# Two score tiles instead of one in every chunk of the gate building, each row whole behind four quads

## The chip, the cores and the metric

The program runs on one core of a Trainium2 chip. The metric is the device time of one execution in microseconds (us), lower is better. The engines are TensorE (PE), VectorE (DVE), ScalarE (ACT), GpSimd (POOL) and SyncE (SP, which here only issues weight loads).

## The reference

Two blocks over 512 tokens of width 1024 in float32. The first block has two layers (feed-forward, mixer, feed-forward), the second one a mixer and then a layer of 16384 experts. Only this last layer, `_peer`, is touched:

```python
qry = (t @ w_q).reshape(n_tok, 8, 2, 128)
scores = einsum("thpd,hpkd->thpk", qry, sub_keys)
s_top, i_top = top_k(scores, 16)              # per half key
cand = s_top[..0..] + s_top[..1..]; best, pos = top_k(cand, 16)
gate = softmax(best)                          # 8 heads x 16 experts a token
act = gelu(tb . u_tab[idx]); out = sum((gate * act) * v_tab[idx])
```

The kernel does not gather experts. It computes the score of all 16384 experts for all tokens as a dense product with u_tab, applies gelu, multiplies by a dense gate matrix that is zero where an expert was not chosen, and takes the dense product with v_tab.

## The kernel before

**Weights.** All weights come as tiles of 128 x 2048 floats (1 MB). SP loads a tile into `raw`, two slots in turn, as soon as the slot's low part has been taken. ACT copies it into `w_hi` in a reduced format (`split_hi`, L427), POOL computes the rest `w_lo = raw - w_hi` in four pieces (L390), and PE forms every product three times: high by high, high by low, low by high (`product`, L925 to L927). A tile of u_tab holds two score rows of 128 experts each; a row is 8 blocks times 3 matmuls, 24 matmuls of 128 x 512, and so a tile is 48. The queue of ACT is in order: `split_hi` of tile n + 2 stands right behind the issue of the store of tile n.

**Groups.** The 128 score rows are 32 groups (`GROUPS`) of four rows, two u tiles and two v tiles each. The scores of the first `AHEAD` = 18 groups, 36 tiles, are computed ahead, before the gates are there: PE fills bank e (0 or 1) with a row (`ahead_row`), ACT applies gelu into `stage` (`stage_row`, L740), and stores the tile of two rows to DRAM (`store_tile`, `s_store`, L745). They are read back per group into `s_in` (L809). The places of the 36 tiles are: 24 between the top-k steps (6 behind each of four key score blocks, `CHOICE_TILES`), 8 in the gate building, one for every chunk, and 4 behind it (`last` to `last + 3`). While those 4 run, the first groups of gates are loaded.

**Gate building.** A quad is four tokens. DVE writes the one-hot operands of a quad (`hots`: four tensor_scalar, L2410, and one tensor_tensor, L2413) into one of four buffers of `hot`, PE makes its gates in one of four banks (`quad`, L1631; the profile shows 8 matmul records for a quad), ACT copies the bank to `g_buf` (L785). DVE waits for quad q - 4 before it overwrites a buffer, PE waits for the copy of quad q - 4 before it overwrites a bank. A chunk is 16 quads (64 tokens); there are 8. PE runs four quads, then half a row (12 matmuls), four times for a chunk. At the end of a chunk ACT issues the store of 4 MB of gates (`g_store`, L791), and right behind it the store of the score tile and `split_hi`:

```python
                        stage_row(CHOICE_TILES * TT + c, half)
                    c_ev.held()
                    act.dma_start(g_store[:, c] ..., g_buf[:, c % 2] ...)
                    store_tile(CHOICE_TILES * TT + c)
```

**Groups of the experts.** An early group (g below `AHEAD`) costs PE two v tiles only (`v_products`), and loads 1 MB of gates, 1 MB of scores and 2 MB of weights. A late group costs PE two u tiles (`s_products`) and two v tiles. DVE multiplies scores by gates (`weigh`, L2441), ACT and DVE split the product (L825, L2448), DVE adds the result to `x` (L2460).

Of the kernel before, what the change touches and what calls it, by code (L numbers as in the profile page):

```python
# [29 lines left out]
TT = TOKENS // P  # L30
# [30 lines left out]
GROUPS = NKEYS // EG  # L61
CHUNK = 64
CHUNKS = TOKENS // CHUNK
AHEAD = 18
AHEAD_TILES = 2 * AHEAD
CHOICE_TILES = 6
QUAD_BUFS = 4
# [48 lines left out]
def build(nc, x_in, weights, gains, small, pool_w, consts, rope, second, level_masks,  # L116
# [3 lines left out]
    with stack:  # L120
# [15 lines left out]
        def sem(name):  # L136
            if name not in sems:
                sems[name] = stack.enter_context(nc.semaphore(name))
            return sems[name]
# [193 lines left out]
        def u_tile(g):  # L333

            return TABLE_AT + (2 * g if g < AHEAD else 4 * g - 2)

        def v_tile(g):

            if g < AHEAD - 1:
                return TABLE_AT + AHEAD_TILES + 2 * g  # L340
# [62 lines left out]
        def _(act):  # L403
# [15 lines left out]
            def split_hi(tile, i=None, per=2):  # L419

                if i is None and tile >= TILES:
                    return
                slot, half = tile % 2, tile // 2
                act.wait_ge(tile_landed[slot], 16 * (half + 1) if i is None else i * (8 * per) + 16 * (half + 1))
                if tile >= 2:
                    act.wait_ge(tile_used, tile - 1 if i is None else i * per + (tile - 1))
                act.activation(w_hi[:, slot, :], raw[:, slot, :], ACT.Copy).then_inc(hi_written, 1)  # L427
# [257 lines left out]
            def experts():  # L685
# [44 lines left out]
                def stage_row(n, e, i=None):  # L730

                    if e == 0:
                        act.wait_ge(sem("s_ahead_done"), n + 1 if i is None else i * 2 + (n + 1))
                        if n >= 2:

                            there = 16 * (n // 2)
                            act.wait_ge(s_stored[n % 2], there if i is None else i * 16 + there)
                    else:
                        act.wait_ge(tile_used, TABLE_AT + n + 1 if i is None else i * 2 + (TABLE_AT + n + 1))
                    c_st.up(act.activation(stage[:, n % 2, e, :], banks[e][:, :], ACT.Gelu))  # L740

                def store_tile(n, i=None):
                    target = n if i is None else act.snap(i * 2 + n)
                    c_st.held()
                    act.dma_start(s_store[target], stage[:, n % 2]).then_inc(s_stored[n % 2], 16)  # L745
                    split_hi(TABLE_AT + n + 2, i)
# [7 lines left out]
                for t in range(TT):  # L754
                    n = CHOICE_TILES * t
# [16 lines left out]
                for c in range(CHUNKS):  # L772
                    for half in range(2):
                        with act.Fori(0, CHUNK // 32) as i:
                            c_ev.loop(i, 4)
                            for b in range(4):
                                q = CHUNK // 4 * c + CHUNK // 8 * half + b
                                at = act.snap(i * 16 + (CHUNK // 2 * half + 4 * b))
                                act.wait_ge(sem("quad_done"), i * 4 + (q + 1))

                                if c >= 2:
                                    act.wait_ge(stored[c % 2], 16 * (c // 2))
                                else:
                                    act.wait_ge(sem("keys_landed"), 32)
                                c_ev.up(act.activation(  # L785
                                    g_buf[:, c % 2, :, bass.ds(at, 4)],
                                    banks[quad_banks[b]][:, :].rearrange("p (t i) -> p i t", t=4), ACT.Copy))
                        c_ev.end(CHUNK // 32)
                        stage_row(CHOICE_TILES * TT + c, half)
                    c_ev.held()  # L790
                    act.dma_start(g_store[:, c].rearrange("g j n -> j g n"),  # L791
                                  g_buf[:, c % 2].rearrange("p (g e) t -> p g (e t)", g=GROUPS)).then_inc(stored[c % 2], 16)
                    store_tile(CHOICE_TILES * TT + c)


                landed = [sem("gates_landed0"), sem("gates_landed1")]
# [2 lines left out]
                def load_group(g, i=None):  # L799
# [3 lines left out]
                    if g >= 2 or i is not None:  # L803
# [3 lines left out]
                                  g_store[source].rearrange("c j n -> j c n")).then_inc(landed[g % 2], 16)  # L807
                    if g < AHEAD:
                        act.dma_start(s_in[:, g % 2].rearrange("p (a e) t -> p a (e t)", a=2),  # L809
# [3 lines left out]
                def chain(g, e, i=None):  # L813
                    at = EG * g + e + 1 if i is None else i * (2 * EG) + (EG * g + e + 1)
                    if g >= AHEAD:

# [3 lines left out]
                        else:  # L820
                            done = 2 * (g - AHEAD) + e // 2 + 1
                            act.wait_ge(sem("s_done"), done if i is None else i * 4 + done)
# [35 lines left out]
                        c.end(trips)  # L858


                last = CHOICE_TILES * TT + CHUNKS
                assert AHEAD_TILES == last + 4
                ahead(last)
                ahead(last + 1)
# [32 lines left out]
            for layer in range(LAYERS):  # L897
                ffn(2 * layer)
                mix(layer)
                ffn(2 * layer + 1)  # L900
            second_mixer()
            experts()

        @block.tensor
        def _(pe):
# [16 lines left out]
            def product(out_ap, slot, blk, m_hi, m_lo, start, stop):  # L922

                cols = slice(blk * P, blk * P + P)
                pe.matmul(out_ap, w_hi[:, slot, cols], m_hi, start=start, stop=False)  # L925
                pe.matmul(out_ap, w_hi[:, slot, cols], m_lo, start=False, stop=False)  # L926
                return pe.matmul(out_ap, w_lo[:, slot, cols], m_hi, start=False, stop=stop)  # L927
# [8 lines left out]
            def wait_tile(tile, i=None, per=2):  # L936
                pe.wait_ge(lo_written, tile + 1 if i is None else i * per + (tile + 1))
# [602 lines left out]
            def experts():  # L1540
# [38 lines left out]
                def ahead_row(n, e, part, i=None):  # L1579

                    tile = TABLE_AT + n
                    if part == 0:
                        if e == 0:
                            wait_tile(tile, i)
                        if n > 0:

                            at = 2 * (n - 1) + e + 1
                            pe.wait_ge(sem("s_staged"), at if i is None else i * 4 + at)
                    for r in range(KB // 2 * part, KB // 2 * (part + 1)):
                        if n == 0 and e == 0 and i is None:  # L1590
                            pe.wait_ge(sem("h_lo_written"), KB * (k + 1) + r + 1)
                        last = product(banks[e][:, :], tile % 2, KB * e + r, h_hi[:, r, :], h_lo[:, r, :],
                                       r == 0, r == KB - 1)
                    if part == 1:
                        (used if e else c_sa).up(last)

                def ahead(n, i=None):
                    for e in range(2):
                        for part in range(2):
                            ahead_row(n, e, part, i)  # L1600

                key_scores(0)
                for t in range(TT):
                    n = CHOICE_TILES * t
# [19 lines left out]
                def quad(q, i=None):  # L1624
                    pe.wait_ge(sem("hot_written"), q + 1 if i is None else i * PER_TRIP + (q + 1))
                    if q >= QUAD_BUFS:

                        at = q - QUAD_BUFS + 1
                        pe.wait_ge(sem("quad_stored"), at if i is None else i * PER_TRIP + at)
                    for n in range(4):  # L1630
                        ins = pe.matmul(banks[quad_banks[q % 4]][:, n * P:n * P + P], hot[:, q % 4, n, 1, :],  # L1631
                                        hot[:, q % 4, n, 0, :], start=True, stop=True)
                    c_quad.up(ins)

                PER_TRIP = 2 * CHUNK // 4

                def two_chunks(c, i=None):

                    for m in range(2):
                        for part in range(4):  # L1640
                            for n in range(4):
                                quad(CHUNK // 4 * (c + m) + 4 * part + n, i)
                            ahead_row(CHOICE_TILES * TT + c + m, part // 2, part % 2, i)

                two_chunks(0)
                with pe.Fori(0, (CHUNKS - 2) // 2) as i:
                    c_quad.loop(i, PER_TRIP)
                    used.loop(i, 2)
                    c_sa.loop(i, 2)
                    two_chunks(2, i)  # L1650
                for c in (c_quad, used, c_sa):
                    c.end((CHUNKS - 2) // 2)


                def s_products(g, i=None):
# [26 lines left out]
                                           w_mix_lo[:, g % 2, e, :], e == 0, e == EG - 1)  # L1682
                        (used if d % 4 == 3 else c_v).up(last)

                for n in range(CHOICE_TILES * TT + CHUNKS, AHEAD_TILES):
                    ahead(n)


# [956 lines left out]
```

## Time and profile before

| | us |
|---|---|
| median of 3 runs | 4459.71 (4449.06 to 4461.06) |
| the profiled execution's own time | 4452.29 |
| its span in the profile | 4450.5 |
| PE busy | 4218.7 (95%) |
| DVE busy | 1950.5 (44%) |
| POOL busy | 1795.3 (40%) |
| ACT busy | 1313.2 (30%) |
| mean granted TensorE clock | 0.974 of full speed |

The span is the time between the first and the last recorded event; the execution's own time has 1.8 us around it. PE's busy time counts a matmul from its start to its modelled end, and neighbours overlap, so the spacing of starts tells the cost of one, not the mean duration.

### The profile page before, as it was taken

The numbers are of one execution on the slowest core, as the hardware profiler recorded it, in microseconds if no ns is written. First come the engines' busy times: TensorE is split into PE (matmuls) and PEld (weight loads), VectorE is DVE, ScalarE is ACT, GpSimd is POOL, SyncE is SP. The second block draws the span as 40 slices with busy tenths as digits, with TensorE's granted clock in tenths as the row PEclk, the third lists the DMA queues.
The fourth block names the chain that finished last, engine by engine and source line by source line (L and its number), as shares of the span: only waits on it lengthen the run. The fifth ranks groups of instructions, "written<-read, shape, count | busy, mean of one in ns | idle before, by whom it ended". The sixth has DMA issues, their size and how long they took to land.

```text
span 4450.5 us, 54686 instructions
## 1 busy us (share of the span) xinstructions
PE 4218.7 (95%) x20004; PEld 3501.2 (79%) x20004; DVE 1950.5 (44%) x3700; ACT 1313.2 (30%) x1599; POOL 1795.3 (40%) x1328
## 2 busy tenths in 40 slices
PE   8999899999999999999987889999888999999998
PEld 6888668888888777887866878787787888888887
DVE  2213443212212443211387763695884666333333
ACT  3222243223222143222231123333333222222322
POOL 4444234444444334444320014445113555554553
PEclk9999999999999999999998999999999999999999
DMA  3222112222222112223110002333456555333332
GB/s 123 95 104 88 64 69 95 94 96 93 95 103 97 67 67 85 94 96 108 57 48 1 1 20 105 109 128 133 154 177 217 193 194 195 126 113 132 113 123 76
DMA packets 127504, 461.30 MB, mean 104 GB/s; under 512 B 8080, under 2 KB 73872, under 8 KB 84752
## 3 DMA queue, kind: packets, MB, share of 16 engines
q1 hardware_dynamic: 48960, 351.29, 22.1%
q10 hardware_dynamic: 78416, 108.22, 7.0%
q8 instruction: 90, 1.47, 0.1%
q14 instruction: 38, 0.31, 0.0%
HBM read 404.96 MB, written 54.53 MB: 103 GB/s over the span
## 4 chain that ended last, share of the span: by engine, by line
issue 51%; POOL 25%; PE 23%; DVE 0%; POOLq 0%; ACT 0%; ACTq 0%; DVEq 0%
POOL w_lo L390 25%; PE bank L925 8%; PE bank L926 8%; PE bank L927 8%; POOLq L394 0%; DVE x L2511 0%; POOLq L397 0%; DVE weighed L2441 0%; DVE w_mix_lo L2448 0%; DVE sq_last L1759 0%; PE bank L967 0%; PE bank L960 0%; ACT stage L740 0%; POOLq L390 0%; DVE sq_last L1760 0%
## 5 line engine op out<-in xcount | busy, mean ns | idle before, releaser
L390 POOL TENSOR_TENSOR w_lo<-raw,w_hi 128x512 fp32r<-128x512 f32 x1324 | 1795.1, 1387 | 2621.7 <-ACT w_hi L427 2621.6
L925 PE MATMUL bank<-h_hi,w_hi 128*128 128x512 f32 x3232 | 1283.6, 397 | 53.6 <-POOL w_lo L390 26.9
L926 PE MATMUL bank<-h_lo,w_hi 128*128 128x512 f32 x3232 | 1267.6, 392 | 0.0
L927 PE MATMUL bank<-h_hi,w_lo 128*128 128x512 f32 x3232 | 1267.5, 392 | 0.0
L427 ACT ACTIVATE w_hi<-raw 128x2048 fp32r<-128x2048 f32 x331 | 632.4, 1911 | 1207.9 <-PE bank L927 1129.8
L925 PEld LDWEIGHTS bank<-h_hi,w_hi 128*128 128x128 f32 x3232 | 613.7, 190 | 189.2 <-issue 50.1
L927 PEld LDWEIGHTS bank<-h_hi,w_lo 128*128 128x128 f32 x3232 | 612.4, 189 | 130.6
L926 PEld LDWEIGHTS bank<-h_lo,w_hi 128*128 128x128 f32 x3232 | 614.0, 190 | 127.4 <-issue 1.8
L925 PE MATMUL bank<-w_mix_hi,w_hi 128*128 128x512 f32 x1024 | 398.4, 389 | 0.9 <-ACT stage L740 0.9
L927 PE MATMUL bank<-w_mix_hi,w_lo 128*128 128x512 f32 x1024 | 398.3, 389 | 0.0
L926 PE MATMUL bank<-w_mix_lo,w_hi 128*128 128x512 f32 x1024 | 398.3, 389 | 0.0
L2460 DVE TENSOR_TENSOR x<-x,bank 128x512 f32<-128x512 f32 x256 | 172.6, 684 | 299.8 <-PE bank L927 298.2
L925 PE MATMUL bank<-act_hi,w_hi 128*128 (+1 forms) x704 | 273.9, 389 | 0.0
L926 PE MATMUL bank<-act_lo,w_hi 128*128 (+1 forms) x704 | 273.9, 389 | 0.0
L927 PE MATMUL bank<-act_hi,w_lo 128*128 (+1 forms) x704 | 273.9, 389 | 0.0
L1774 DVE SCALAR_TENSOR_TENSOR x<-bank,x 128x512 f32<-128x512 f32 x56 | 38.1, 681 | 453.5 <-PE bank L927 453.5
L1802 DVE TENSOR_TENSOR up_s<-bank,rstd 128x512 f32<-128x512 f32 x88 | 60.9, 692 | 383.1 <-PE bank L927 382.9
L925 PEld LDWEIGHTS bank<-w_mix_hi,w_hi 128*128 128x128 f32 x1024 | 192.2, 188 | 41.4 <-issue 1.3
L927 PEld LDWEIGHTS bank<-w_mix_hi,w_lo 128*128 128x128 f32 x1024 | 192.2, 188 | 39.8
L926 PEld LDWEIGHTS bank<-w_mix_lo,w_hi 128*128 128x128 f32 x1024 | 192.2, 188 | 39.8
L456 ACT ACTIVATE act_hi<-up_s 128x512 f32 (+1 forms) x88 | 55.6, 631 | 461.2 <-DVE up_s L1804 461.2
L1631 PE MATMUL bank<-hot 128*128 128x128 f32 x1024 | 139.2, 300 | 39.1 <-ACT g_buf L785 32.7
(372 smaller groups left out, 4442.8 us busy)
## 6 DMA issues: line engine op xcount, KB each, us to landing
raw<-weights SPq DMA_DIRECT2D x331, 1024.0 KB, 4.8
g_store<-g_buf ACTq DMA_DIRECT2D x8, 4096.0 KB, 13.6
g_in<-g_store ACTq DMA_DIRECT2D x32, 1024.0 KB, 5.5
s_store<-stage ACTq DMA_DIRECT2D x36, 512.0 KB, 3.2
s_in<-s_store ACTq DMA_DIRECT2D x18, 1024.0 KB, 7.5
x<-x_in SPq DMA_DIRECT2D x1, 2048.0 KB, 10.4
out<-x SPq DMA_DIRECT2D x8, 256.0 KB, 2.2
keys_sb<-keys ACTq DMA_DIRECT2D x1, 1024.0 KB, 4.7
```

The costliest lines, as they stand in the source:

```text
L390: ins = pool.tensor_tensor(w_lo[:, slot, cols], raw[:, slot, cols], w_hi[:, slot, cols].bitcast(F32), ALU.subtract)
L427: act.activation(w_hi[:, slot, :], raw[:, slot, :], ACT.Copy).then_inc(hi_written, 1)
L456: c_act_hi.up(act.activation(act_hi[:, at, :], prod[:, :], ACT.Copy))
L925: pe.matmul(out_ap, w_hi[:, slot, cols], m_hi, start=start, stop=False)
L926: pe.matmul(out_ap, w_hi[:, slot, cols], m_lo, start=False, stop=False)
L927: return pe.matmul(out_ap, w_lo[:, slot, cols], m_hi, start=False, stop=stop)
L1631: ins = pe.matmul(banks[quad_banks[q % 4]][:, n * P:n * P + P], hot[:, q % 4, n, 1, :], hot[:, q % 4, n, 0, :], start=True, stop=True)
L1774: c_x.up(dve.scalar_tensor_tensor(x[:, n, :], banks[n][:, :], scale, x[:, n, :], ALU.mult, ALU.add))
L1802: c_us.step(dve.tensor_tensor(up_s[:, :], banks[up_bank][:, :], rstd[:, :], ALU.mult))
L2460: c_x.up(dve.tensor_tensor(x[:, d, :], x[:, d, :], banks[4 + d % 4][:, :], ALU.add))
```

## The change

Every chunk now carries two score tiles, one for each half of its quads. A whole row (24 matmuls) stands behind every four quads, where half a row stood. So 16 tiles lie in the gate building instead of 8, `AHEAD` goes from 18 to 22 (44 tiles ahead), and four groups turn from late ones into early ones; their 8 u tiles are no longer computed in the late phase. The order of the weight tiles on the host follows `AHEAD`. On ACT the store of a score tile and the `split_hi` behind it now come once for each half, before the store of the gates, no longer behind it. PE's loop covers one chunk in place of two.

```diff
-AHEAD = 18
+AHEAD = 22
...
-                        stage_row(CHOICE_TILES * TT + c, half)
+                        n = CHOICE_TILES * TT + 2 * c + half
+                        stage_row(n, 0)
+                        stage_row(n, 1)
+                        store_tile(n)
                     c_ev.held()
                     act.dma_start(g_store[:, c].rearrange("g j n -> j g n"),
                                   g_buf[:, c % 2].rearrange("p (g e) t -> p g (e t)", g=GROUPS)).then_inc(stored[c % 2], 16)
-                    store_tile(CHOICE_TILES * TT + c)
...
-                last = CHOICE_TILES * TT + CHUNKS
+                last = CHOICE_TILES * TT + 2 * CHUNKS
...
-                PER_TRIP = 2 * CHUNK // 4
-
-                def two_chunks(c, i=None):
-
-                    for m in range(2):
-                        for part in range(4):
+                PER_TRIP = CHUNK // 4
+
+                def chunk_quads(c, i=None):
+
+                    for half in range(2):
+                        for e in range(2):
                             for n in range(4):
-                                quad(CHUNK // 4 * (c + m) + 4 * part + n, i)
-                            ahead_row(CHOICE_TILES * TT + c + m, part // 2, part % 2, i)
-
-                two_chunks(0)
-                with pe.Fori(0, (CHUNKS - 2) // 2) as i:
+                                quad(CHUNK // 4 * c + 8 * half + 4 * e + n, i)
+                            for part in range(2):
+                                ahead_row(CHOICE_TILES * TT + 2 * c + half, e, part, i)
+
+                chunk_quads(0)
+                with pe.Fori(0, CHUNKS - 1) as i:
...
-                    two_chunks(2, i)
+                    chunk_quads(1, i)
...
-                for n in range(CHOICE_TILES * TT + CHUNKS, AHEAD_TILES):
+                for n in range(CHOICE_TILES * TT + 2 * CHUNKS, AHEAD_TILES):
                     ahead(n)
```

## Rows read from the trace of the kernel before

**Rows 1.** The page, its first part: busy time of each engine.

```profile
PE 4218.7 (95%) x20004; PEld 3501.2 (79%) x20004; DVE 1950.5 (44%) x3700; ACT 1313.2 (30%) x1599; POOL 1795.3 (40%) x1328
```

**Rows 2.** Windows: stretch, length, busy by engine, granted clock, DMA share, GB/s.

```profile
3128.40:3378.10 249.70, 217.05 (x1379) 198.26 (x1379) 211.84 (x615) 93.98 (x147) 34.73 (x28) 0.92 0.47 162
3389.00:3394.60 5.60, 0.00 (x0) 0.00 (x1) 0.00 (x0) 3.41 (x4) 4.99 (x5) 0.80 0.89 327
3394.60:3402.30 7.70, 7.70 (x24) 6.18 (x25) 0.00 (x0) 0.00 (x0) 4.88 (x4) 0.70 0.59 196
...
3430.60:3823.00 392.40, 392.38 (x1731) 324.94 (x1732) 238.95 (x278) 110.49 (x111) 206.00 (x144) 1.00 0.53 189
3823.00:4430.00 607.00, 607.00 (x2680) 502.62 (x2679) 201.92 (x225) 171.01 (x168) 307.24 (x220) 1.00 0.32 114
```

**Rows 3.** Waits from 3090 to 3390 us: total us, times, longest.

```profile
ACT w_hi L427 <- issue: 64.1, 8, 8.9
...
PE bank L1631 <- ACT g_buf L785: 32.7, 7, 4.9
```

**Rows 4.** Timeline of PE, one quiet quarter: start, us, line.

```profile
3177.01 3.73 PE L1631 MATMUL bank<-hot 128*128 128x128 f32 x32
3180.49 0.48 PE L925 MATMUL bank<-h_hi,w_hi 128*128 128x512 f32 x1
...
3183.31 0.94 PE L1631 MATMUL bank<-hot 128*128 128x128 f32 x7
```

**Rows 5.** Timeline of DVE, the same quarter, POOL idle.

```profile
3180.29 1.10 DVE L2410 TENSOR_SCALAR hot<-numbers,chosen 128x128 f32<-128x128 f32 x4
...
3181.92 1.11 DVE L2410 TENSOR_SCALAR hot<-numbers,chosen 128x128 f32<-128x128 f32 x4
```

**Rows 6.** Timeline of ACT and its DMA issues behind a chunk.

```profile
3183.52 0.39 ACTq L791 DMA_DIRECT2D g_store<-g_buf  x1
3184.14 7.92 ACTq L745 DMA_DIRECT2D s_store<-stage  x1
3192.16 1.91 ACT L427 ACTIVATE w_hi<-raw 128x2048 fp32r<-128x2048 f32 x1 [8.05 <-issue]
3193.97 2.04 ACT L785 ACTIVATE g_buf<-bank 128x512 f32 x4
```

**Rows 7.** Timeline of PE behind that chunk.

```profile
3194.69 5.30 PE L1631 MATMUL bank<-hot 128*128 128x128 f32 x32 [4.92 <-ACT g_buf L785]
```

**Rows 8.** Timeline of ACT behind the end of a whole tile.

```profile
3115.07 0.60 ACT L740 ACTIVATE stage<-bank 128x512 f32<-128x512 f32 x1 [4.84 <-PE bank L927]
```

**Rows 9.** Timeline of POOL at the start of the building.

```profile
3118.12 5.40 POOL L390 TENSOR_TENSOR w_lo<-raw,w_hi 128x512 fp32r<-128x512 f32 x4 [5.84 <-ACT w_hi L427]
```

**Rows 10.** Timeline of DVE beside it: two quads from one row to the other.

```profile
3117.69 3.02 DVE L2410 TENSOR_SCALAR hot<-numbers,chosen 128x128 f32<-128x128 f32 x4
...
3124.90 1.10 DVE L2410 TENSOR_SCALAR hot<-numbers,chosen 128x128 f32<-128x128 f32 x4
```

**Rows 11.** Timeline of ACT's DMA issues behind the last chunk.

```profile
3378.15 0.39 ACTq L791 DMA_DIRECT2D g_store<-g_buf  x1
3378.77 8.75 ACTq L745 DMA_DIRECT2D s_store<-stage  x1
...
3409.40 0.40 ACTq L806 DMA_DIRECT2D g_in<-g_store  x1
```

**Rows 12.** Timeline of PE behind the last chunk.

```profile
3394.60 0.79 PE L925 MATMUL bank<-h_hi,w_hi 128*128 128x512 f32 x1 [5.62 <-POOL w_lo L390]
```

**Rows 13.** Timeline of ACT in the early groups: split of two neighbouring tiles.

```profile
3768.20 1.92 ACT L427 ACTIVATE w_hi<-raw 128x2048 fp32r<-128x2048 f32 x1 [4.67 <-PE bank L927]
...
3779.08 1.92 ACT L427 ACTIVATE w_hi<-raw 128x2048 fp32r<-128x2048 f32 x1 [8.44 <-PE bank L927]
```

**Rows 14.** DMA issues from 3117 to 3378 us: KB each, median us to landing.

```profile
g_store<-g_buf ACTq DMA_DIRECT2D x7, 4096.0 KB, 13.6
raw<-weights SPq DMA_DIRECT2D x8, 1024.0 KB, 4.8
```

More of the change, by code:

```diff
@@ L1649, in experts @@
                     c_sa.loop(i, 2)
-                    two_chunks(2, i)
+                    chunk_quads(1, i)
                 for c in (c_quad, used, c_sa):
-                    c.end((CHUNKS - 2) // 2)
+                    c.end(CHUNKS - 1)
                 def s_products(g, i=None):
```

## The prediction

> **What bounds the kernel now.** I read the page first: PE is busy for 95% of the span and DVE, the next one, for 44% [rows 1]. The windows by stage then show where the missing PE time lies. Through the early groups (3431 to 3823 us) and the late ones (to 4430) PE is busy from end to end at the full granted clock [rows 2]: nothing but PE's own work counts there. The gate building is different: of 249.7 us from the first row of scores to the last, PE shows 217.1 busy at a granted clock of 0.92, and behind it stand 5.6 us with no matmul and then a row of 24 matmuls that took 7.7 us at a clock of 0.70 [rows 2]. The waits of the stage name the holes: PE waits 32.7 us in 7 pieces for ACT's copies to g_buf, and ACT's split_hi stands 64.1 us in 8 pieces behind "issue", which is a time in its own queue [rows 3]. The timeline of ACT says which: g_store (4 MB) is issued in 0.39 us, and the next DMA issue, s_store, holds ACT for 7.92 us; only then come split_hi and the copies of the next quads [rows 6]. PE finds no free bank for 4.92 us, and its next 32 quad records take 5.30 us instead of 3.73 [rows 7, 4]. A part of them ran at the lower of the two clock levels, 1.2 for 2.4 GHz: the grant falls behind a pause of PE.
>
> What would the stage be without these holes? In a quiet quarter of a chunk four quads take 3180.49 - 3177.01 = 3.48 us and the half row 2.82, a quarter 6.30 us [rows 4]. From the first row to the end of the last one there are 31 such quarters and one more half row: 31 x 6.30 + 2.82 = 198.1 us. The stage has 249.7, so 51.6 us are lost; 0.5 of these I leave as the slow first matmuls behind the start, which nothing in the change touches. DVE needs 3181.92 - 3180.29 = 1.63 us for a quad [rows 5], 6.52 for four, so it is nearly as long as PE's quarter.
>
> **The change part by part.** (a) *Eight tiles leave the late phase.* The splits of two neighbouring tiles are 10.88 us apart where PE is dense [rows 13], and late groups are as dense [rows 2]. So 8 x 10.88 = 87.0 us go there. The four groups' v tiles, gates and DVE work stay.
>
> (b) *They come into the building.* Each of 32 quarters gets 12 matmuls more, a quarter of a tile or 2.72 us: 32 x 2.72 = 87.0 us. PE's work as such is only moved; a gain must come from the holes. The quarter becomes 9.02 us.
>
> (c) *The store of the scores goes ahead of g_store.* Behind g_store ACT now goes straight to the copies. Its next DMA issue is half a chunk later, 18.0 us, while the block of an issue behind g_store ended within 9.4 us (0.62 + 8.75 at the longest) [rows 11]. So the 51.1 us of holes go, if nothing takes their place: the stage is 31 x 9.02 + 5.54 + 0.5 = 285.7 us, 36.0 longer than now.
>
> (d) *The tail.* The hole of 5.62 us in front of the second tile behind the building [rows 12] has the same cause: the last s_store issue holds split_hi for 8.75 us, then POOL is late. It goes, and with it the slow row: 7.7 - 5.44 = 2.3 us. Together -7.9.
>
> (e) *ACT's work moved.* Each half now has two gelus, one issue, one split_hi. The stage copy starts some 0.2 us behind a row's end, and POOL, which waits for split_hi, started 3.05 us behind that copy [rows 8, 9]. So ACT is free some 3.3 us behind the row; the copies of the four quads that PE meanwhile makes take 2.04 us [rows 6], are there by 5.4 and needed at 9.0. Behind ACT stand PE's banks, POOL and DVE; all have over 3 us. Without that cover each half would cost its excess, 16 times. The weights: the load of a tile lands in 4.8 us, gates in 13.6 [rows 14]; a tile's slot now turns over in 18.0 us a tile, not the 10.88 of the dense stages. At the end, g_store is issued some 3.4 us after the last row, and the load of its gates (now 31.3 us behind the issue [rows 11]) some 23 us after that row, 19.5 us behind it: above the 13.6.
>
> (f) *DVE.* The four one-hot buffers let DVE build four quads while PE does the row: 6.52 us against 9.02. But POOL's split now comes twice as often. Where they met at the start of the building, two quads took 7.21 us from row to row instead of 3.26: 3.95 us lost in a POOL stretch of 5.40 [rows 9, 10]. In the new quarter with POOL (from 3.2 us behind a row's end, for some 5), DVE starts when the first quad is done, at 3.48 / 4 = 0.87 and 0.2 more, has 2.1 us of work done when POOL starts, some 1 in POOL's stretch, and ends the fourth quad at 11.6. PE asks for it at 9.02 + 3 x 0.87 = 11.6. It fits to a hair; over a half DVE needs 13.04 + 3.95 = 17.0 of 18.04. The bounds: nothing, or, if DVE gets nothing done beside POOL for 5.0 us, 1 us per tile, 16 us. I take 2, since the row with the measured overlap fits.
>
> The Trainium skill (SBUF — State Buffer, Who interferes with whom) speaks against this change here: a VectorE operation with two SBUF inputs, as hots' tensor_tensor, and a GpSimd one that reads SBUF lock each other out for a whole instruction. By that rule alone, full exclusion for the whole stretch, the sum would be 14 us worse; the row above shows that DVE got a part of its work through.
>
> (g) *Four more early groups.* Each loads 4 MB in 21.8 us of PE; the 18 of now run at a PE share of 100% with 189 GB/s [rows 2], to their end. I cost it at nothing; the cover is the time of two v tiles. PE's loop runs 7 times rather than 3; through the loops of the groups PE shows no hole [rows 2].
>
> **Sum** on the profiled execution: -87.0 + 36.0 - 7.9 + 2 = -56.9 us: a span of 4393.6 and a time of 4452.3 - 56.9 = 4395.4. The median of the runs is 7.4 us above the profiled one, and the sum laid on it gives 4402.8. I say 4398.
>
> **The rivals.** *DVE and POOL collide more than the start row shows.* For: the quarter with POOL has no slack for its last quad, and the two quads at the start lost 3.95 us. Against: over a half DVE still has 1 us to spare. With (f)'s upper bound of 16 us for my 2 it gives 4412, and if each of 16 pauses also costs PE 1 us at its lower clock, as the quads behind a hole do now (5.30 for 3.73) [rows 4, 7], 4428.
>
> *The block stays.* g_store may take longer beside twice the weights, or hold whatever ACT issues next. For: the issues right behind a g_store were held, 7.92 us in a chunk and 8.75 at the last [rows 6, 11]. Against: the next one is now 18 us away. If the same 51 + 8 us stand again, the time is 4457, no change: the added rows only move.
>
> *Slower: the quads wait for their hots in a row.* If four buffers are too few for a gap as long as a whole row, each quarter becomes the row plus DVE's pace instead of PE's. It ends the gain at 59 / 32 = 1.8 us per quarter, and it is slower by 13 us from 2.3: a quarter of 11.3 us. DVE has 6.52 in a quarter and, even if it stands still in all of POOL's stretch, 5 more in every second one, a mean of 9.0. Fully serial (5.44 + 6.52 + 0.87 = 12.8 a quarter) is 3.8 x 32 = 122 us more: 4520. Against it: in the quiet quarter DVE went from quad to quad while PE did its half row [rows 4, 5].
>
> **How the numbers follow.** Forecast 0.80 (4388 to 4408, the holes gone, contention 0 to some us, and the spread of 12 us of the three runs), collision 0.11, block stays 0.06, serial hots 0.03. The predicted time is the forecast's. The range takes in the collision up to 4424, and 4386 below, for a sum without contention on the profiled run's level. About 0.3% (13 us) is what a measurement of this kernel can tell from no change. Faster by more: 0.80 + 0.11 + a part of the block, 0.92; within: 0.05; slower: 0.03.
>
> **What would show it.** In the profile after: PE's wait for g_buf gone, quarters of 9.0 us, a first-to-last row of 286 us (a collision shows as PE waits for hot instead), granted clock 1.00 through the building, no s_store issue above 1 us, an s_store issue 18 us behind g_store, no wait for w_lo behind the building, and a late phase 87 us shorter. The prediction is wrong if PE waits for hot or for g_buf at the end of each half, if the early groups beyond the 18th wait for loads, or if weights land late beside g_store.

## The result and the profile after

The change makes the kernel faster by 1.2%: 4405.26 us median of 4 runs (4399.87 to 4410.98) against 4458.59 us (4449.06 to 4461.06), a ratio of 0.9882 with a 95% interval of 0.9869 to 0.9896. I had said 4398, in 4386 to 4424. The runs of either kernel lie on two levels some 10 us apart (one of four on the lower level before, two of four after); between like levels the difference is 49 us, so the medians show a little too much.

The medians differ by 53.3 us, but the two profiled executions differ by 41.3 us of span. The first place to read is therefore one that the change does not touch: the first matmul of the first key scores. The rows are of the view of one tile (`keys_sb`): duration min/median/max in ns, first and last start in us. Before:

```profile
L1572 PE MATMUL bank<-keys_sb,qry x128: 274/275/582, 2817.1 to 2975.6; 128*128 128x128 f32 x128
```

and after:

```profile
L1574 PE MATMUL bank<-keys_sb,qry x128: 274/275/579, 2825.3 to 2983.9; 128*128 128x128 f32 x128
```

The same work before this place took 8.2 us longer in the profiled execution of the changed kernel. So for all traces below I compare the stretch from the first quad to the end of the span. Its first start is in the view of the tile `hot`, before:

```profile
L1631 PE MATMUL bank<-hot x1024: 270/275/582, 3117.8 to 3375.1; 128*128 128x128 f32 x171
```

and after:

```profile
L1633 PE MATMUL bank<-hot x1024: 270/275/582, 3126.2 to 3426.1; 128*128 128x128 f32 x171
```

Before, the stretch is 4450.5 - 3117.8 = 1332.7 us, after 4409.2 - 3126.2 = 1283.0: 49.7 us less.

The windows of the changed kernel by stage answer to [rows 2] (stretch, length, busy PE, PEld, DVE, ACT, POOL with counts, granted clock, DMA share, GB/s):

```profile
3136.80:3431.75 294.95, 290.23 (x1763) 256.56 (x1763) 264.58 (x615) 113.53 (x171) 86.75 (x60) 1.00 0.53 180
3431.75:3475.30 43.55, 43.55 (x193) 35.84 (x191) 8.19 (x7) 14.29 (x16) 21.47 (x16) 1.00 0.92 314
3476.20:3955.00 478.80, 478.65 (x2112) 396.50 (x2113) 294.14 (x342) 134.24 (x135) 252.14 (x176) 1.00 0.53 190
3955.00:4389.00 434.00, 434.00 (x1916) 359.49 (x1915) 143.66 (x161) 122.30 (x120) 217.57 (x156) 1.00 0.32 111
```

The gate building, from its first row of scores to its last, grew from 249.7 to 294.95 us. Its granted clock is 1.00 where it was 0.92. The four tiles behind it run without a hole, 43.55 us for 4 x 10.88; the 5.6 us without a matmul and the slow row of before are gone. The early groups are as dense as they were, now for 22 groups.

The timeline of ACT at the end of a chunk answers to [rows 6]:

```profile
3171.39 0.34 ACTq L745 DMA_DIRECT2D s_store<-stage  x1
3171.84 1.91 ACT L427 ACTIVATE w_hi<-raw 128x2048 fp32r<-128x2048 f32 x1 [0.47 <-ACT stage L740]
3171.86 0.40 ACTq L794 DMA_DIRECT2D g_store<-g_buf  x1
3173.66 2.04 ACT L785 ACTIVATE g_buf<-bank 128x512 f32 x4
...
3190.05 0.35 ACTq L745 DMA_DIRECT2D s_store<-stage  x1
```

The score tile's store goes in 0.34 us, the gates' store behind it, and the four waiting copies follow at once. The next issue comes 18.2 us behind the gates' store and is not held (0.35 us).

The timeline of PE over one half of a chunk answers to [rows 4]:

```profile
3151.91 3.73 PE L1633 MATMUL bank<-hot 128*128 128x128 f32 x32
3155.40 0.48 PE L927 MATMUL bank<-h_hi,w_hi 128*128 128x512 f32 x1
...
3160.94 2.84 PE L1633 MATMUL bank<-hot 128*128 128x128 f32 x24
3164.09 1.16 PE L1633 MATMUL bank<-hot 128*128 128x128 f32 x8 [0.31 <-DVE hot L2416]
3165.00 0.47 PE L927 MATMUL bank<-h_hi,w_hi 128*128 128x512 f32 x1
...
3170.57 3.73 PE L1633 MATMUL bank<-hot 128*128 128x128 f32 x32
```

The first quarter is 3160.94 - 3151.91 = 9.03 us, as worked out. The second is 9.63: its burst breaks after three quads (24 records), and the fourth waits for DVE. The profile counts 0.31 us of wait from the modelled end of the quad before; from start to start the quarter is 0.6 us too long. A half is 18.66 us and not 18.04, 0.6 us more, fifteen times. The timelines of DVE and of POOL at that place show why:

```profile
3153.23 1.11 DVE L2413 TENSOR_SCALAR hot<-numbers,chosen 128x128 f32<-128x128 f32 x4 [2.43 <-PE bank L1633]
...
3154.86 4.34 DVE L2413 TENSOR_SCALAR hot<-numbers,chosen 128x128 f32<-128x128 f32 x4
...
3159.72 2.08 DVE L2413 TENSOR_SCALAR hot<-numbers,chosen 128x128 f32<-128x128 f32 x4
...
3163.96 1.10 DVE L2413 TENSOR_SCALAR hot<-numbers,chosen 128x128 f32<-128x128 f32 x4
```

```profile
3155.17 5.78 POOL L390 TENSOR_TENSOR w_lo<-raw,w_hi 128x512 fp32r<-128x512 f32 x4 [23.29 <-ACT w_hi L427]
```

DVE starts 1.32 us behind the row's end (3151.91), does one quad, and then the next two groups of four tensor_scalar take 4.34 and 2.08 us instead of 1.10: 4.2 us lost in POOL's 5.78. So its fourth quad is done at 3163.96, 12.05 us behind the row's end, where PE asks at 11.6.

The waits from 3090 to 3480 us (total, times, longest), against [rows 3]:

```profile
PE bank L1633 <- DVE hot L2416: 11.2, 18, 3.5
```

PE's wait for g_buf is no longer in the list; 18 waits for hot stand there: three at the very start, which were there before, and one in each of the fifteen halves behind them. ACT's split_hi no longer waits behind "issue".

### The profile page after: what moved, and what is told of

It is laid out like the page before. It is cut to its first block, busy times and chain, and to the rows that moved or that the text cites. A ratio compares the mean times of both kernels' runs of the same rounds, so it can differ in the third digit from the quotient of the medians.

```text
span 4409.2 us, 54714 instructions
## 1 busy us (share of the span) xinstructions
PE 4210.2 (95%) x20004; PEld 3492.4 (79%) x20004; DVE 2000.4 (45%) x3700; ACT 1307.7 (30%) x1599; POOL 1804.0 (41%) x1328
## 4 chain that ended last, share of the span: by engine, by line
issue 47%; PE 25%; POOL 24%; DVE 2%; DVEq 1%; POOLq 0%; ACT 0%; ACTq 0%
POOL w_lo L390 24%; PE bank L927 8%; PE bank L929 8%; PE bank L928 8%; DVE hot L2413 1%; PE bank L1633 1%; DVE hot L2416 1%; DVEq L2413 0%; POOLq L394 0%; DVE x L2514 0%; POOLq L397 0%; DVE weighed L2444 0%; DVE w_mix_lo L2451 0%; DVEq L2416 0%; DVE sq_last L1762 0%
## 5 line engine op out<-in xcount | busy, mean ns | idle before, releaser
L2413 DVE TENSOR_SCALAR hot<-numbers,chosen 128x128 f32<-128x128 f32 x512 | 207.6, 465 | 23.9 <-PE bank L1633 23.8
## 6 DMA issues: line engine op xcount, KB each, us to landing
g_store<-g_buf ACTq DMA_DIRECT2D x8, 4096.0 KB, 18.3
```

What stands on the lines that cost most here:

```text
L2413: dve.tensor_scalar(hot[:, q % 4, n, 0, :], numbers[:, :], chosen[:, 0, at], chosen[:, 2, at], ALU.is_equal, ALU.mult)
```

## The experiments

All stretches below are from the first quad to the end of the span of the profiled execution: 1332.7 us for the kernel before, 1283.0 for the changed one. Ratios are against the kernel before.

### One edit on the kernel before: the order of the stores

```diff
+                    store_tile(CHOICE_TILES * TT + c)
                     c_ev.held()
                     act.dma_start(g_store[:, c] ..., g_buf[:, c % 2] ...)
-                    store_tile(CHOICE_TILES * TT + c)
```

> The kernel before with one edit: the last score tile of a chunk is stored ahead of the gates, not behind them; one tile a chunk and half rows stay. Measured from the first quad to the end of the span, the kernel before takes 1332.7 us and the changed one 1283.0. Theory (the holes are cut short by VectorE as soon as the blocked issue is gone): VectorE needs 16 x 1.63 = 26.1 us for a chunk and loses about 4.2 beside GpSimd's split, 30.3 in all, against 32.1 a chunk now; with the 7.9 us of the tail the stretch loses about 20, to 1312 us. Rival (the working of the prediction: PE sets the pace of the quarters, 6.30 us, once the block is gone): 1332.7 - 51 - 8 = 1274 us.

Measured: ratio 0.9945 (0.9931 to 0.9958), 4433.91 us; the first quad starts at 3124.1 in a span of 4432.3, a stretch of 1308.2 us. That is 24.5 less, near the 20 of the theory and far from the 59 of the rival. The window of the building in this kernel shows the new bound:

```profile
3134.70:3366.70 232.00, 213.83 (x1378) 193.70 (x1378) 228.03 (x615) 93.90 (x147) 38.39 (x28) 0.95 0.53 174
```

DVE is busy 228.0 of 232.0 us. With the block gone, half rows leave PE quarters of 6.30 us, and DVE can't feed quads at that pace. PE still pauses, now for DVE, and its clock still falls for a part (0.95).

### One edit on the changed kernel: the gates' store ahead of the second tile's

```diff
                         stage_row(n, 1)
-                        store_tile(n)
+                        if half == 0:
+                            store_tile(n)
                     c_ev.held()
                     act.dma_start(g_store[:, c] ..., g_buf[:, c % 2] ...)
+                    store_tile(n)
```

> The changed kernel with one edit: at the end of a chunk the gates are stored ahead of the second score tile, as in the kernel before; two tiles a chunk and whole rows stay. Theory (the block of the issue behind the gates holds ScalarE 8 us longer, the row of 5.4 us hides a part): ScalarE copies the first quad some 11.3 us behind a row's end, PE wants its bank at 9.0, so 2.8 us a chunk in 7 chunks and 8 us at the tail: 1283 + 28 = 1311 us from the first quad to the end. Rival (the extra row alone fills the holes and the order is worth only the tail): 1291 us. Rival (the order is worth all that was lost): 1283 + 59 = 1342 us.

Measured: ratio 0.9951 (0.9938 to 0.9965), 4435.26 us; 4433.0 - 3122.4 = 1310.6 us, where the theory said 1311. The timeline of ACT shows the held issue again, that of PE what is left of it:

```profile
3210.31 0.39 ACTq L795 DMA_DIRECT2D g_store<-g_buf  x1
3210.93 7.82 ACTq L745 DMA_DIRECT2D s_store<-stage  x1
```

```profile
3210.10 3.73 PE L1635 MATMUL bank<-hot 128*128 128x128 f32 x32
3221.39 3.81 PE L1635 MATMUL bank<-hot 128*128 128x128 f32 x32 [2.10 <-ACT g_buf L785]
```

The quarter with the hold is 11.29 us instead of 9.02: a whole row hides 5.4 us of it, and PE stands 2.10 us where it stood 4.92. The waits of this kernel have 15.8 us of PE for g_buf in seven pieces (1.8 to 3.6 each), and 4.6 us for w_lo behind the building. That the number came out to the microsecond is in part luck, as the starts of PE's quarters show. Behind four of the seven holes the granted clock falls (0.84 over the quarter from 3301.09, which takes 10.77 us, and 1.00 over the one from 3221.39, which takes 9.11), and this costs some 8 us that the theory did not have. In turn the holds of the quarters sum to some 17 us, where the theory had 19.6, and seven of the waits for hot are gone (11 for 18), some 4 us; the tail must then be near 7 us, where it had 8.

The four kernels together, as stretches:

| | one tile, half rows | two tiles, whole rows |
|---|---|---|
| gates' store first | 1332.7 | 1310.6 |
| scores' store first | 1308.2 | 1283.0 |

The order alone gives 24.5 us, the rows alone 22.1, both 49.7.

### The rows spread finer

```diff
                     for half in range(2):
-                        for e in range(2):
-                            for n in range(4):
-                                quad(CHUNK // 4 * c + 8 * half + 4 * e + n, i)
-                            for part in range(2):
-                                ahead_row(CHOICE_TILES * TT + 2 * c + half, e, part, i)
+                        for part in range(4):
+                            for n in range(2):
+                                quad(CHUNK // 4 * c + 8 * half + 2 * part + n, i)
+                            ahead_row(CHOICE_TILES * TT + 2 * c + half, part // 2, part % 2, i)
```

> The changed kernel with the rows spread finer: half a row behind every two quads instead of a whole row behind every four. Same work, same order of the stores. Theory (PE waits 0.6 us in each half because VectorE, slowed beside GpSimd, is late with the fourth quad of a burst, though it has time enough in the mean, 17.3 of 18.04 us): with the quads asked for in pairs the wait goes, 15 x 0.62 = 9.3 us less, 1274 us from the first quad to the end; about 0.2% off the time. Rival (VectorE has no time left in the mean, or ScalarE's copies are late for pairs): 1283 us or more.

Measured: ratio 0.9870 (0.9855 to 0.9885), 4400.03 us; 4395.6 - 3123.3 = 1272.3 us, 10.7 less than the changed kernel, where 9.3 had been forecast. The bursts in the timeline of PE are 4.52 us apart without a break:

```profile
3133.34 1.95 PE L1633 MATMUL bank<-hot 128*128 128x128 f32 x16
3137.86 1.95 PE L1633 MATMUL bank<-hot 128*128 128x128 f32 x16
```

Four of them are 18.08 us for a half. PE's waits for hot are two, 5.9 us, both at the start. DVE has the time in the mean; only a burst of four asked for the last quad too early.

### Three tiles in a chunk

AHEAD is 26, and PE's loop becomes (with ACT's stores in the same order; the lines that go are left out):

```diff
+                        for q, rows in enumerate(((0,), (1, 2), (3,), (4, 5))):
+                            for n in range(4):
+                                quad(CHUNK // 4 * (c + m) + 4 * q + n, i)
+                            for row in rows:
+                                for part in range(2):
+                                    ahead_row(tile + row // 2, row % 2, part, i, 6)
```

> The changed kernel carried one step on: three score tiles in every chunk, AHEAD 26, rows 1, 2, 1, 2 behind the four bursts of four quads. Theory (a tile moved into a stage that PE bounds is neutral, its 10.88 us go in one place and come in the other): VectorE has 23.5 us for a half and PE no longer waits for hot, so the 9.3 us go and nothing else does: 1274 us from the first quad to the end. Rival (each tile moved in still takes a hole away, as the first eight seemed to): another 40 to 50 us less, 1235. Rival (the early groups or the DMA queues get crowded): 1283 or more.

Measured: ratio 0.9880 (0.9864 to 0.9895), 4404.98 us; 4404.9 - 3127.2 = 1277.7 us. Eight tiles more moved into the building save no 40 us: of the 87.0 us taken from the late phase 5.3 remain as a gain. The theory of 1274 was near, but not for all of its reason: where one row only stands behind a burst, the next burst still breaks.

```profile
PE bank L1641 <- DVE hot L2426: 8.0, 10, 2.9
```

These are ten waits of PE for hot; the changed kernel had 18. The eight that went are worth 8 x 0.62 = 5.0 us, nearly the whole 5.3: the eight tiles themselves gain nothing.

### The gates' store in two

On the kernel before, `g_store` of a chunk is issued as two DMAs of 16 groups, 2 MB each:

```diff
+                    for part in range(2):
+                        act.dma_start(g_store[gs, c] ..., g_buf[:, c % 2, es] ...)
-                    act.dma_start(g_store[:, c] ..., g_buf[:, c % 2] ...)
```

> The kernel before with the 4 MB store of a chunk's gates issued as two stores of 2 MB, one behind the other; the score tile's store follows as before. It measures the hold of the issue by itself. Theory (an issue is held until the DMA in front of it on this queue has been worked off for the most part, at the rate seen, 8.3 us for 4 MB): the second gates store is held some 4 us and the score store some 4 us more, the sum stays near 8.3 us, and the stretch from the first quad to the end stays at 1333 us. Rival (a fixed hold behind any large store): about 8 us twice, 16 in the sum, and the stretch grows by some 50 us.

Measured: 4458.84 us in one run, beside 4457.36 of before; 4457.0 - 3123.4 = 1333.6 us. The stretch stays, as the theory said, and no fixed hold came twice. The hold is not shared out in halves, though. The timeline of ACT behind the second chunk and behind the third:

```profile
3189.41 2.48 ACTq L794 DMA_DIRECT2D g_store<-g_buf  x2
3191.92 7.62 ACTq L745 DMA_DIRECT2D s_store<-stage  x1
...
3223.66 2.36 ACTq L794 DMA_DIRECT2D g_store<-g_buf  x2
3226.06 5.98 ACTq L745 DMA_DIRECT2D s_store<-stage  x1
```

Both gates' stores are through in 2.4 us, where the theory had some 4 for the second alone, and the third issue is held for 5.9 to 7.6 us. The hold ends 8.4 us behind the start in the third chunk and 8.2 to 8.6 in five of the others; the second chunk (10.1) and the last one (9.5) stand out. In the kernel before it ends after 8.2 to 8.5 us in seven chunks and 9.4 in the last. So the hold ends about as long behind the start as before, whether one issue or two carry the 4 MB. What the queue counts is left open.

### The choices of the last token tile one score tile earlier

With the pairs of quads, and on PE (the loop of score tiles ahead of it makes one trip less for this token tile):

```diff
+                    if t == TT - 1:
+                        ahead(n + 4)
                     pe.wait_ge(sem("selected"), t + 1)
                     ... # three transposes of sel
                     c_t.up(ins)
+                    if t == TT - 1:
+                        ahead(n + 5)
```

> The kernel with half rows behind pairs of quads, and one edit more: the last token tile's choices are transposed one score tile earlier, so that VectorE builds its first four one-hot operands while PE still has a tile of scores to do. Theory (PE's two waits for hot at the start, 5.9 us, and the slow clock behind them come from VectorE's late start beside GpSimd): the waits go and, counted from a place ahead of the building, 6 to 8 us with them; against the kernel with pairs about 0.15% less, 4393 us or so where that one had 4400. Rival (the choices are not ready a tile earlier): PE waits for them instead, no change or slower.

Measured: ratio 0.9848 (0.9834 to 0.9861), 4390.22 us, the fastest of all. The stretch from the first quad, 4388.2 - 3121.4 = 1266.8 us, is 5.5 less than with the pairs alone; from the first key score on, a mark ahead of the building, it is 4388.2 - 2823.3 = 1564.9 against 4395.6 - 2822.5 = 1573.1, 8.2 less. PE has no wait for hot left.

### GpSimd's split in eight pieces, and in two

```diff
-PIECES = 4
+PIECES = 8
```

> The changed kernel with GpSimd's split of a tile in eight pieces instead of four, all else the same. Theory (VectorE and GpSimd take turns by whole instructions, so VectorE gets one instruction through for each piece): with twice as many turns VectorE loses about half of the 4.2 us it loses now in a split, the quads are in time and PE's 0.6 us in each half go: 1274 us from the first quad to the end, if eight pieces cost GpSimd not over 7 us where four cost 5.0 alone. Rival (they share a bandwidth and not turns): VectorE's loss stays at 4 us or grows with GpSimd's longer time, 1283 us or more.

> The changed kernel with GpSimd's split in two pieces instead of four. Theory (turns by whole instructions): VectorE gets fewer instructions through in a split and loses 4.5 to 5 us instead of 4.2; PE's wait in each half grows from 0.6 to about 1 us, 1283 + 15 x 0.4 = 1289 us from the first quad to the end. Rival (bandwidth shared): no change, 1283.

Measured, eight: ratio 0.9875 (0.9860 to 0.9890), 4402.6 us, 4402.3 - 3125.3 = 1277.0 us. Two: 0.9879 (0.9864 to 0.9894), 4406.83 us, 4406.1 - 3119.5 = 1286.6 us. `PIECES` holds for all stages of the kernel, so only the stretch is compared. The intervals of the ratios don't tell these two apart; the stretches, each from one profiled execution, move the way the theory said, by about two thirds of it each. The timeline of DVE beside eight pieces, one after the other:

```profile
3208.14 2.69 DVE L2413 TENSOR_SCALAR hot<-numbers,chosen 128x128 f32<-128x128 f32 x4
...
3211.35 2.85 DVE L2413 TENSOR_SCALAR hot<-numbers,chosen 128x128 f32<-128x128 f32 x4
3214.12 1.23 DVE L2416 TENSOR_TENSOR hot<-numbers,chosen 128x512 f32<-128x512 f32 x1
```

and beside two:

```profile
3204.74 5.50 DVE L2413 TENSOR_SCALAR hot<-numbers,chosen 128x128 f32<-128x128 f32 x4
```

DVE loses 1.6 + 1.7 + 0.6 = 3.9 us beside eight pieces (POOL's stretch 6.36 us), 4.2 beside four (5.78) and 4.4 beside two (4.86). So the loss did not halve with eight, and this step of the theory was wrong. That the two engines take turns by whole instructions is seen in the instructions one by one. The view of the tiles `hot` and `w_lo` beside two pieces (min/median/max in ns):

```profile
L2413 DVE TENSOR_SCALAR hot<-numbers,chosen x4: 336/1414/2575, 3204.7 to 3209.9; 128x128 f32<-128x128 f32 x4
L390 POOL TENSOR_TENSOR w_lo<-raw,w_hi x2: 2442/2448/2455, 3205.0 to 3207.4; 128x1024 fp32r<-128x1024 f32 x2
```

Two of the four tensor_scalar run at their usual 0.34 us, and two stand for as long as a piece of POOL lasts. Over the building the longest tensor_scalar is 0.92 us beside eight pieces, 1.48 beside four and 2.59 beside two, where POOL's shortest piece is 0.73, 1.33 and 2.44. It grows with the piece, which a shared bandwidth would not give. With more pieces DVE gets more instructions through (in the rest of POOL's stretch, 2.5, 1.6 and 0.5 us), but each of these lengthens POOL's stretch: the tensor_tensor of 3159.12 in the changed kernel runs its usual 0.68 us, and POOL's piece beside it takes 1.87 instead of 1.33. So the loss stays near 4 us (6.36 - 2.5, 5.78 - 1.6, 4.86 - 0.5). PE's half went from 18.66 to 18.30 us with eight and to 18.84 with two, in fifteen halves 5.4 us less and 2.7 more.

More than four one-hot buffers would take the wait from another side; this wasn't tried.

## Why the prediction came out right

**(a) Eight tiles less, -87.0.** Borne out where PE is dense: the tile is 10.88 us in all kernels (43.55 for four behind the building), and the late phase of 10 groups is without a hole.

**(b), (c) The building, +36.0.** The quarter of 9.02 us came as worked out (9.03), and the held issue went. But the building grew by 45.3 and not by 36.0, and the 9.3 between them are (f). One thing was put wrongly: "So the 51.1 us of holes go" holds for the order of the stores only in the company of (b). Alone the order gives 24.5 us for the whole stretch, since DVE is then busy 98% of the building. The added row slows PE's quarter to above DVE's pace; that is what turned the holes into work. The other way round, the rows alone hide only 22.1, since 1.8 to 3.6 us of each hold still reach PE. A further tile is then moved and no more: three tiles a chunk gave 5.3 us, and that through fewer waits for hot.

**(d) The tail, -7.9.** Its hole and its slow row are gone, and both are back in part (4.6 us of wait) when the gates' store goes first again.

**(e) ACT's work and the DMAs, 0.** No wait of PE for ACT's copies is left. The weights land in 4.8 us as before. So the rival "the block stays" did not come. One figure was off without harm: a gates' store now lands in 18.3 us and not 13.6. The rows are

```profile
g_store<-g_buf ACTq DMA_DIRECT2D x7, 4096.0 KB, 18.3
raw<-weights SPq DMA_DIRECT2D x15, 1024.0 KB, 4.8
```

and the load of the first group's gates was issued 21.8 us behind the last one (19.5 had been worked out). That cover is down to some 3.5 us. The rival had thought of "twice the weights" here; the runs put it down to the order of the stores. With one tile and the new order a gates' store lands in 18.4 us, with two tiles and the old order in 13.6.

**(f) DVE beside POOL, +2.** This is the term that was mis-sized: it measured 15 x 0.62 = 9.3 us. I had the fourth quad at 11.6 us behind the row, "to a hair"; it came at 12.05, because DVE started at 1.32 and not 1.07, and lost 4.2 us and not 3.95. Two quarters of a microsecond, in a place with no slack and fifteen repeats, made 7 us. The upper bound of 16 held. The finer spread (-10.7) and the pieces (-6.0 with eight, +3.6 with two) show that this wait is the cause. A sign that I had named for a wrong prediction, that PE waits for hot in each half, is therefore in the trace (in the second burst of the half): the first rival, the collision, came about half way, 7.3 us of its 14, without the loss at the lower clock (the building has 1.00). The forecast "contention 0 to some us" was too kind, and its range took this in.

The Trainium skill (SBUF — State Buffer, Who interferes with whom) names the lock between the two engines. The trace agrees instruction by instruction (a tensor_scalar of 0.33 us took up to 1.48), but the prediction's reading of it over a whole stretch was too dear, since DVE got instructions through between two pieces of POOL. And I had named the tensor_tensor; in the quarter shown the instructions that stood were tensor_scalar, while the tensor_tensor held POOL.

**(g) Four more early groups, 0.** Borne out: PE is busy 478.65 of 478.80 us through them.

The third rival, serial hots, did not come either: the first quarter of each half is 9.03 us.

The sum was -56.9 and the trace has -49.7; of the 7.2 between them (f) alone makes 7.3, so the other terms hold to within rounding. The mechanism was right and one term too small. That 4405.26 lies only 2.5 us above the sum as laid on the median (4402.8) is in part luck: the medians differ by 53.3 us, 3.6 more than the trace, through the mix of runs named with the result, and the median of before came out 1.1 us lower with its fourth run.

## What to carry to other kernels

In these kernels the issue right behind a 4 MB store was held some 8 us, and with it everything behind in ACT's queue; an issue 10 or 18 us behind it was not (0.34 us). So put small stores and the work that others wait for ahead of a large store, and let the next issue be far away. Removing a hole uncovers the engine that is next in pace: fill the stage with PE work from elsewhere until PE is the slowest there, and stop, since a tile moved beyond that point was neutral here. Ask for another engine's products in small, even bursts: then the mean decides, and not the last one of a burst (bursts of two quads for four took 10.7 us off).

## What the runs showed of the hardware

- The issue behind a 4 MB store was held 7.5 to 9.3 us in ACT's queue (16 places in two kernels); split into two stores of 2 MB, the issues of these took 1.8 to 3.0 us together and the third was held 5.9 to 7.6 us.
- VectorE lost 4.4, 4.2 and 3.9 us beside GpSimd's subtraction in 2, 4 and 8 pieces, and GpSimd's own stretch grew from 4.86 to 5.78 and 6.36 us. One fp32 tensor_scalar stood up to 2.59, 1.48 and 0.92 us, about the length of one piece.
- The profiled executions differ before the changed part is reached: the first key score starts at 2817.1 us in the trace of before and at 2821.6 to 2825.4 in the seven others that are the same up to there. What makes this difference is open.
